# Hyena token sums inside the global attention, and six spectrum loads issued from the Pool queue

## What is computed, cut to what matters

```python
def even_mixer(p, p_ctx, ..., need_ctx):
    aq, ak, av, hu, ag, hg = split_cols(p, EVEN_SPLITS)
    q = apply_rope(rms_norm(heads(aq, N_Q_HEADS), q_norm), cos, sin)
    k = apply_rope(rms_norm(heads(ak, N_KV_HEADS), k_norm), cos, sin)
    y_a = global_gqa(q, k, v, k_c, v_c)
    y_b = hyena_branch(hu, conv_w, conv_b, w1, b1, w2, b2, freq, w3, d_skip)
    y = jnp.concatenate([y_a * silu(ag), y_b * silu(hg)], axis=-1)

def hyena_branch(u, ...):
    uc = centred_depthwise_conv(u, conv_w, conv_b)
    parts = jnp.split(uc, HYENA_ORDER + 1, axis=-1)
    z = parts[0]
    for o in range(HYENA_ORDER):                 # two orders
        z = parts[o + 1] * bidir_long_conv(z, filt[:, o, 0], filt[:, o, 1], d_skip[o])
    return z

def bidir_long_conv(z, h_fwd, h_bwd, d_skip):
    zf = jnp.fft.rfft(z, n=2 * n, axis=1)
    tf = jnp.fft.rfft(taps, n=2 * n, axis=0)
    return jnp.fft.irfft(zf * tf[None], n=2 * n, axis=1)[:, :n] + z * d_skip
```

## Time and profile before

| | |
|---|---|
| runs | 3074.2, 3077.98, 3078.12 us |
| profiled execution | 3075.42 us, its span 3073.6 us |
| global attention of layer 0 | about 439.9 to 547.3 us of the span |
| Hyena stage of layer 0 | 547.36 to 636.2 us |
| granted PE clock, mean | 0.975 |

### The profile page before, as it was taken

The page is one execution under the profiler, slowest core; times in us unless marked ns, Lnnn a source line. Parts: engine busy times, 40 slices in busy tenths (PEclk is TensorE's granted clock), DMA queues, the critical chain, the costliest instruction groups (busy, mean ns, idle before and its releaser), DMA issues.

```text
span 3073.6 us, 39670 instructions
## 1 busy us (share of the span) xinstructions
PE 2877.1 (94%) x15492; PEld 2226.1 (72%) x15492; DVE 1670.3 (54%) x3179; ACT 1072.0 (35%) x1872; POOL 448.9 (15%) x401
## 2 busy tenths in 40 slices
PE   5899989999998899999999899999999999899998
PEld 2488874789974486475887688887566788678887
DVE  6855667754677745735345642426755334563344
ACT  3433345124146522535222431322454323332231
POOL 3300013321005431302020000000222011000000
PEclk8999999999999999999999999999999999899999
DMA  5443320232232043011323222234111323133231
GB/s 174 151 128 110 97 76 1 83 97 95 69 100 48 25 125 86 19 60 55 103 82 137 69 96 96 96 96 105 31 46 33 103 89 103 55 104 102 88 104 69
DMA packets 224928, 261.75 MB, mean 85 GB/s; under 512 B 12818, under 2 KB 187010, under 8 KB 224616
## 3 DMA queue, kind: packets, MB, share of 16 engines
q1 hardware_dynamic: 207328, 203.93, 21.7%
q0 software_dynamic: 12544, 45.08, 4.2%
q10 hardware_dynamic: 4872, 10.21, 1.5%
HBM read 245.04 MB, written 13.11 MB: 84 GB/s over the span
## 4 chain that ended last, share of the span: by engine, by line
PE 54%; DVE 8%; issue 2%; ACT 1%; DMA 1%; POOL 0%; SPq 0%; DVEq 0%; ACTq 0%; POOLq 0%
PE PS L349 30%; PE PS L3762 10%; PE PS L156 3%; PE PS L3661 2%; PE PS L1227 2%; PE PS L1216 2%; PE PS L1203 1%; DVE S L1256 1%; DVE S L2646 1%; DVE HL L297 1%; DVE S L1284 1%; DVE S L2642 1%; DMA S<-in_w_in 1%; PE PS L2486 1%; PE PS L3422 1%
## 5 line engine op out<-in xcount | busy, mean ns | idle before, releaser
L349 PE MATMUL PS<-xT,HL 128*128 128x512 f32 (+1 forms) x3552 | 790.3, 383 | 12.0 <-DVE xT L2498 4.7
L297 DVE TENSOR_TENSOR HL<-S,HL 128x2048 fp32r<-128x2048 f32 (+2 forms) x204 | 423.8, 2082 | 645.0 <-ACT HL L290 644.8
L349 PEld LDWEIGHTS PS<-xT,HL 128*128 128x128 f32 x3552 | 642.9, 187 | 152.4 <-DVE xT L2498 5.4
L290 ACT ACTIVATE HL<-S 128x2048 fp32r<-128x2048 f32 (+2 forms) x204 | 351.5, 1729 | 661.1 <-PE PS L349 284.9
L3762 PE MATMUL PS<-HL,hd 128*128 128x512 f32 x1536 | 350.2, 389 | 0.1
L3762 PEld LDWEIGHTS PS<-HL,hd 128*128 128x128 f32 x1536 | 288.1, 188 | 60.8 <-PE PS L3762 1.0
L1315 ACT ACTIVATE S<-S,S 128x256 f32<-128x256 f32 (+5 forms) x292 | 189.1, 648 | 184.8 <-DVE S L1256 177.5
L1350 POOL TENSOR_SCALAR S<-S,S 128x512 f32<-128x512 f32 (+4 forms) x104 | 180.0, 1731 | 382.2 <-DVE S L1271 221.7
L1216 PEld LDWEIGHTS PS<-S,S 128*128 128x128 f32 (+1 forms) x1048 | 116.9, 144 | 145.1 <-issue 50.0
L1216 PE MATMUL PS<-S,S 128*128 128x128 f32 (+1 forms) x1048 | 175.2, 296 | 41.5 <-DVE S L1284 18.5
L349 PE MATMUL PS<-h_high,HL 128*128 128x512 f32 (+1 forms) x768 | 201.2, 348 | 0.1
(11 more groups left out here) (412 smaller groups left out, 3910.8 us busy)
## 6 DMA issues: line engine op xcount, KB each, us to landing
S<-in_mlp_w_up SPq DMA_DIRECT2D x32, 1024.0 KB, 5.4
S<-in_mlp_w_down SPq DMA_DIRECT2D x32, 1024.0 KB, 5.1
S<-in_w_in SPq DMA_DIRECT2D x28, 1024.0 KB, 5.3
S<-in_w_ada SPq DMA_DIRECT2D x24, 1024.0 KB, 5.2
S<-in_w_gate SPq DMA_DIRECT2D x24, 1024.0 KB, 5.1
S<-in_w_in SPq DMA_DIRECT2D x36, 512.0 KB, 5.2
S<-in_w_mix_out SPq DMA_DIRECT2D x8, 1024.0 KB, 5.0
spectra<-S POOLq DMA_DIRECT2D x24, 256.0 KB, 4.9
```

Of the source, the lines that this page charges most:

```text
L290: m = a.activation(high, raw, ACT.Copy)
L297: m = v.tensor_tensor(low, raw, high.bitcast(F32), ALU.subtract)
L349: m = pe.matmul(dst, l[x], r[y], start=(i == 0 and j == 0), stop=(i == n - 1 and j == 2))
```

## The change

`paired_attention` gets an argument `scored` that collects the semaphore value of each scores step. `token_sums` is taken apart into `sum_steps` (four for a long half, one for a short half), each with a DVE drain wait in front. The ten steps of order 0's halves become "extra" steps 6 to 15 of the global attention: DVE runs each right behind the norm of its number. After the attention's instructions Pool waits for the last scores and issues six of the 24 spectrum loads (order 0, k = 0, 2, 1); ACT keeps 18. `TR` and `TI` of k = 0, 1, 2 lie where queries and keys were; k = 3 of `TI` overlaps a transposed-row buffer and stays on ACT behind the barrier. The reduced diff:

```diff
-    def paired_attention(jobs, P, PT, banks=1, ready=(), extra=None):
+    def paired_attention(jobs, P, PT, banks=1, ready=(), extra=None, scored=None):
...
...
+                if scored is not None:
+                    scored.append(sc[n, i][2])
...
-    paired_attention(jobs, tile_pairs(tiles), ..., banks=2, ready=t_k + t_q)
-    f = barrier()
...
-    for o in range(2):
-        for k in range(4):
-            a.dma_start((TR, TR1)[o][:, k, :], spectra[o, :, 2 * k]).then_inc(*ld_T[o][k].up())
-            a.dma_start((TI, TI1)[o][:, k, :], spectra[o, :, 2 * k + 1]).then_inc(*ld_T[o][k].up())
...
+        def apart():
             v.wait_ge(*vl.at)
             v.tensor_tensor(y[:, 2:4, :], u.tiles(0, 2), u.tiles(2, 4), ALU.add).then_inc(*vl.step())
             v.tensor_tensor(y[:, 4:6, :], u.tiles(0, 2), u.tiles(2, 4), ALU.subtract).then_inc(*vl.event())
+        def even():
             v.wait_ge(*vl.at)
             v.tensor_tensor(y0, y1r, y1i, ALU.add).then_inc(*vl.step())
             v.tensor_tensor(y4, y1r, y1i, ALU.subtract).then_inc(*vl.event())
+        def odd_imag():
+            v.wait_ge(*vl.at)
             v.scalar_tensor_tensor(y3i, y1i, -c8, z[2], ALU.mult, ALU.add).then_inc(*vl.step())
             v.wait_ge(*vl.at)
             v.scalar_tensor_tensor(y1i, y1i, -c8, z[2], ALU.mult, ALU.subtract).then_inc(*vl.step())
+        def odd_real():
+            v.wait_ge(*vl.at)
             v.scalar_tensor_tensor(y1r, y2i, c8, z[0], ALU.mult, ALU.add).then_inc(*vl.event())
             v.scalar_tensor_tensor(y3r, y2i, -c8, z[0], ALU.mult, ALU.add).then_inc(*vl.event())
+        return [((2,), apart), ((0,), even), ((), odd_imag), ((1, 3), odd_real)]
...
+    first_halves = halves(0)
+    early_sums = [None] * 6 + [(u, *x) for u in first_halves[0] + first_halves[1] for x in sum_steps(u)]
...
+    scored = []
+    paired_attention(jobs, tile_pairs(tiles), ..., banks=2, ready=t_k + t_q,
+                     extra=dict(steps=[early_sum(i) for i in range(len(early_sums))], plan=plan_early, tensor=lambda: None),
+                     scored=scored)
+    g.wait_ge(*scored[-1])
+    for k in (0, 2, 1):
+        g.dma_start(TR[:, k, :], spectra[0, :, 2 * k]).then_inc(*ld_T[0][k].up())
+        g.dma_start(TI[:, k, :], spectra[0, :, 2 * k + 1]).then_inc(*ld_T[0][k].up())
+    f = barrier()
+    for o in range(2):
+        for k in range(4):
+            if o or k == 3:
+                a.dma_start((TR, TR1)[o][:, k, :], spectra[o, :, 2 * k]).then_inc(*ld_T[o][k].up())
+                a.dma_start((TI, TI1)[o][:, k, :], spectra[o, :, 2 * k + 1]).then_inc(*ld_T[o][k].up())
...
     for o in range(2):
+        M, C = halves(1) if o else first_halves
-        if o == 0:
-            for u in M + C:
-                token_sums(u)
-        else:
+        if o:
             for u, was in zip(M + C, last):
                 u.ready = was
```

More of the change, by code:

```diff
@@ L1976, in program @@
                                    final=yfinal(yT[:, pair, q00 * 128:(q00 + nq) * 128], nq * 128)))
-    tiles = grid(BIG + 21504, 12, 768) + grid(XR, 4, 768)
-    paired_attention(jobs, tile_pairs(tiles), grid(BIG + 3840, 4, 512) + grid(XR + 4608, 2, 512), banks=2, ready=t_k + t_q)
-    f = barrier()
     TR, TI = sb(BIG, 4, 512), sb(BIG + 2048, 4, 512)
@@ L1991, in program @@
     ld_T = [[Loads(nc, f"spectrum{o}_{k}") for k in range(5)] for o in range(2)]
-    for o in range(2):
-        for k in range(4):
-            a.dma_start((TR, TR1)[o][:, k, :], spectra[o, :, 2 * k]).then_inc(*ld_T[o][k].up())
-            a.dma_start((TI, TI1)[o][:, k, :], spectra[o, :, 2 * k + 1]).then_inc(*ld_T[o][k].up())
-        for k in range(2):
-            a.dma_start((tr, tr1)[o][:, k, :], spectra[o, :, 8 + 2 * k]).then_inc(*ld_T[o][4].up())
-            a.dma_start((ti, ti1)[o][:, k, :], spectra[o, :, 9 + 2 * k]).then_inc(*ld_T[o][4].up())
     class Half:
@@ L2015, in tiles, with sum_steps, both @@
             return UC[:, self.t0 + t0:self.t0 + t1, c:c + 256]
-    def token_sums(u):
+    def sum_steps(u):
         y = u.y
[L2020 to L2023, removed]
+        if not u.long:
+            z = [u.tiles(t, t + 1)[:, 0, :] for t in range(2)]
+            def both():
+                v.wait_ge(*vl.at)
+                v.tensor_tensor(y[:, 0, :], z[0], z[1], ALU.add).then_inc(*vl.step())
+                v.tensor_tensor(y[:, 1, :], z[0], z[1], ALU.subtract).then_inc(*vl.event())
+            return [((0,), both)]
+        y0, y4, y1r, y1i, y2r, y2i, y3r, y3i = [y[:, i, :] for i in range(8)]
+        z = [u.tiles(t, t + 1)[:, 0, :] for t in range(4)]
+        def apart():
             v.wait_ge(*vl.at)
@@ new lines, in plan_sums, with token_sums, halves @@
+    def plan_sums(u, made):
+        for k in made:
+            u.ready[k] = dv.next()
+            if not u.long:
+                u.ready[1] = u.ready[0]
+    def token_sums(u):
+        u.ready = {}
+        for made, step in sum_steps(u):
+            plan_sums(u, made)
+            step()
+    def halves(o):
+        T = ((TR, TI, tr, ti), (TR1, TI1, tr1, ti1))[o]
+        return ([Half(0, 4, h, T[0:2], ld_T[o], sb(HL + 3072 + h * 2048, 8, 256)) for h in range(2)],
+                [Half(4, 2, h, T[2:4], [ld_T[o][4]] * 2, sb(HL + 7168 + h * 512, 2, 256)) for h in range(2)])
@@ new lines, in program, with plan_early, early_sum, step @@
+    first_halves = halves(0)
+    early_sums = [None] * 6 + [(u, *x) for u in first_halves[0] + first_halves[1] for x in sum_steps(u)]
+    def plan_early(i):
+        if early_sums[i]:
+            plan_sums(*early_sums[i][0:2])
+    def early_sum(i):
+        def step(dve, act):
+            if dve and early_sums[i]:
+                early_sums[i][2]()
+        return step
+    tiles = grid(BIG + 21504, 12, 768) + grid(XR, 4, 768)
+    scored = []
+    paired_attention(jobs, tile_pairs(tiles), grid(BIG + 3840, 4, 512) + grid(XR + 4608, 2, 512), banks=2, ready=t_k + t_q,
+                     extra=dict(steps=[early_sum(i) for i in range(len(early_sums))], plan=plan_early, tensor=lambda: None),
+                     scored=scored)
@@ new lines, in program @@
+    g.wait_ge(*scored[-1])
[8 more added lines that the diff above has]
+                a.dma_start((TI, TI1)[o][:, k, :], spectra[o, :, 2 * k + 1]).then_inc(*ld_T[o][k].up())
+        for k in range(2):
+            a.dma_start((tr, tr1)[o][:, k, :], spectra[o, :, 8 + 2 * k]).then_inc(*ld_T[o][4].up())
+            a.dma_start((ti, ti1)[o][:, k, :], spectra[o, :, 9 + 2 * k]).then_inc(*ld_T[o][4].up())
@@ L2194, in program @@
     for o in range(2):
-        T = ((TR, TI, tr, ti), (TR1, TI1, tr1, ti1))[o]
-        M = [Half(0, 4, h, T[0:2], ld_T[o], sb(HL + 3072 + h * 2048, 8, 256)) for h in range(2)]
-        C = [Half(4, 2, h, T[2:4], [ld_T[o][4]] * 2, sb(HL + 7168 + h * 512, 2, 256)) for h in range(2)]
-        if o == 0:
-            for u in M + C:
-                token_sums(u)
-        else:
+        M, C = halves(1) if o else first_halves
+        if o:
             for u, was in zip(M + C, last):
```

## The result

| | before | after |
|---|---|---|
| median of 12 runs each | 3076.81 us | 3082.44 us (3078.66 to 3088.91) |
| profiled span | 3073.6 us | 3076.8 us |
| attention: first scores on PE to ACT's first spectrum issue | 107.39 us | 117.72 us |
| Hyena stage: that issue to PE's first matmul of the gate | 88.82 us | 86.81 us |

The ratio is 1.0025, interval 1.0014 to 1.0035: slower by 4.3 to 10.8 us. The two stretches together are 8.3 us longer (+10.33 - 2.01). The profiled spans differ by 3.2 us only: the profiled execution of the kernel after is the fastest of its twelve, and outside of these stretches one execution is not like the next (runs of the kernel before alone lie between 3068 and 3085 us).

What follows compares the result with a forecast made beforehand. It took PE, in a loop with DVE, to bound the attention and ACT's DMA issues to hold the Hyena stage's third product. Attention cost 8.7 less stage gain 2.9 gave +5.8 us: 3083.8 us, range 3075.5 to 3091.0.

Steps and rivals of the forecast that it cites:

- The loop of PE and DVE, place by place: Attention: sums behind norms delay PE, 1.9 us at three places, 1.5 at two, 0 behind norm 1; sum 8.7 us.
- the last place: Attention, behind norms 2 and 3 of job 3: the short halves' sums make PE 1.9 us late.
- the case without standing: Attention: cost of the sums if none of them stands beside Pool's scaling, given as 6.4 us.
- The standing beside Pool: Attention: a sum step behind norms 0, 1, 2 stands 0.57 us during Pool's scaling, nothing behind norm 3.
- the rival in which the sum stands for all of Pool's record: Attention: sums stand 1.4 us longer at seven places, 9.8 us; total +15.0 us, 3093.0 us; chance 0.12.
- The low clock: Rival, attention: PE's waits lower its granted clock, 1.7 us per stretch, two 3.4, total 3087 us; chance 0.17.
- my case: Whole kernel: attention cost less stage gain, +5.8 us, with 2.2 to about 8; chance 0.50.
- The Hyena stage: Third product starts 10.9 us behind ACT's first issue instead of 13.8, a gain of 2.9 us.
- The same issues took: Hyena stage: ACT's 19th issue started 10.03 us behind the first in the trace before, taken for the 18 issues left.
- from 561.15 on the chain runs to the stage's end: Hyena stage: from the third product on, DVE, Pool, ACT run without waiting on PE; stage gains what that product gains.
- Six issues on Pool for nothing: Before the stage: six load issues of 0.54 us each, 3.3 us on Pool, which is free then, cost nothing.
- The rival that the attention hides the sums: Attention: DVE's idle time takes the sums, only the last place costs 1.9 us; result -2.4, 3075.6 us; chance 0.14.

Runs made afterwards that it cites:

- e2: The change with the sums back at the Hyena stage's start, six loads still issued by Pool; ratio to the kernel before 0.9995.
- e5: The change with the sums back at the stage's start and order 1's twelve loads issued behind the first half's ACT instructions; ratio to before 1.0001.
- e1: The change with all 24 spectrum loads left on ACT, the sums still in the attention; ratio to the kernel before 1.0025.
- e7: The change with only three M0 sum steps in the attention, behind norm 1 of jobs 1 to 3, and order 1's loads issued later; ratio to before 0.9986.
- e4: The change with each sum step ahead of its norm instead of behind it; one run, attention 115.10 us, stage 86.53 us.
- e3: The change with ACT issuing order 1's twelve loads later, behind the first half's `forward`; ratio to the kernel before 1.0010.
- e6: The change with the short halves' sums back in the Hyena stage, M0's and M1's eight steps left in the attention; ratio to before 1.0013.
- e10: The change without the drain waits it added to the sums of order 1; ratio to the kernel before 1.0024.
- e9: e7 with the short halves' sums behind norm 3 of jobs 1 and 2, and without the added drains in order 1; ratio to before 0.9981.
- e8: e7 with M0's odd_real ahead of the stage's products and the other remaining sums between them; ratio to the kernel before 0.9992.

## Why the prediction was right, and where it was not

The median moved by 5.6 us where I said 5.8. That agreement is in part luck: in the two stretches the cost is 8.3 us, and the interval of 4.3 to 10.8 us holds both numbers. In all eight kernels with a sum in the attention that were run several times, the median lies 1.0 to 3.3 us lower than the two stretches say, in the two without (e2, e5) the two agree within 0.2 us. Each of these stretches is from one trace, and only e1's lies outside of its own interval (its trace has 1.0 us of low clock of its own); whether something outside of the stretches gets shorter, no trace shows. By step:

- **The loop of PE and DVE, place by place.** 1.9 us behind norms 2 and 3 of jobs 1 and 2: measured 1.84 and 1.85. 1.5 behind norm 0: 1.51 and 1.55. Nothing behind norm 1: 0 both times, and e7 shows it alone. 1.9 for the last place: 2.10 at first, since the second norm still stood 0.18 us there (L1279 0.80 instead of 0.62), which I had counted as regained; 0.31 of it comes back at the next tile, so I was wrong that nothing is won back there. Sum 8.5 for 8.7. (The 6.4 us that I named for the case without standing does not come out of my own terms: 8.7 less 0.57 at five places is 5.9.)
- **The standing beside Pool**, 0.57 us at seven places and nothing behind norm 3: measured 0.58 and 0. In every case DVE went on 1.17 to 1.19 us behind Pool's start, of a record of 2.63. e4 shows that it goes with Pool. So the rival in which the sum stands for all of Pool's record falls, and with it 9.8 us. The Trainium skill, SBUF — State Buffer, section "Who interferes with whom", has the later of the two instructions blocked fully until the other is through; that one waits for the other the traces bear out, that it waits until the recorded end they do not (by that the attention would be some 9 us longer than it is). Why DVE goes on after 1.2 us, whether Pool is by then through with what it shares with DVE and the record merely runs on, no run shows.
- **The low clock**, a rival with 0.17: it came, once, and cost 1.6 us (1.7 said). It came on top of my case, not in its place, so it belonged into the sum as a further term. A stretch of 3.41 us at 1.2 GHz inside jobs 3 and 4 stands in all five traces that have the sums of M0 and M1 behind their norms in jobs 2 and 3 (81 us from the first scores in after; 71 in e1, e3, e6 and e10, 1.6 us there too, right behind PE's wait for L1286 in job 3), and in none of the seven others. PE's waits of 1.73 us for L1286 are in these five only; e4 has waits of 1.67 and 1.99 us at other places and no such stretch, so the length of a wait does not decide it alone. So it goes with these sums; which wait brings it, and why it comes later in after, stays open. The stretch at the attention's tail is there before and after alike.
- **The Hyena stage**, 2.9 us said, 2.0 measured. The mechanism was right (e3: the third product follows ACT's issues; e1 and e2: neither half of the change does it alone). The size failed twice. "The same issues took" 10.03 us: they took 10.4, since the slowest of them took 1.43 us (1.15 before) and the last 0.65 (0.45). And the step "from 561.15 on the chain runs to the stage's end" was followed for what is taken out of the stage, not for what the new form of `token_sums` puts in: the second order's sums run through it too, with four more drains, some 0.45 us (e10). I had priced the drains in the attention only.
- **Six issues on Pool for nothing:** confirmed, 551.54 to 554.8 with the stage starting at 557.64; e2's attention is unchanged.
- **The rival that the attention hides the sums** falls: of ten steps only the two behind norm 1 were hidden.

The difference of 8.3 and 5.8 is then 1.6 of clock, 0.9 of the stage, and about 0.15 by which the attention was already later before the first sum, less 0.15 for the places.

## What to carry to other kernels

Idle time of an engine is free only where the instruction behind it has slack: here DVE idled 2.2 us in 10, and of two gaps one (ahead of the fourth scores) took a 1.4 us step for nothing and the other, with 0.55 us usable, charged all above that to PE. Put moved work into the gap that a timeline shows, step by step, and look at what Pool is doing beside it; e9 moves five of the same ten steps, with the late loads and without the added drains, and wins 0.2%; moving all ten costs 0.25%, and still 0.1% with late loads (e3). Before moving work out of a stage's start, list what else gates its first dependent step, and when a helper is rewritten for one caller, price its new waits at every other caller. And before putting work between others, ask who waits for it: in e8 it was PE, the engine with the least slack.

## What the runs showed of the hardware that was not expected

- Standing beside the other engine goes both ways. Pool's 128x256 TENSOR_TENSOR took up to 1.23 instead of 0.73 us beside DVE's sums in e8, and these 1.22 instead of 0.68.
- Four waits of DVE for its own last instruction made the chain that runs over DVE 0.41 to 0.51 us longer (e10, e9), some 0.1 us each.
- Issues from ACT's queue follow each other at 0.48 us as a rule, but in ten of the twelve traces one of the 18 or 24 takes 1.0 to 2.4 us, and ACT's compute instructions behind them wait for all of it (10.44 us in after, 11.1 in e10).
